# The vector engine parts weight blocks in place of POOL: RWKV projections and adding stages

## The chip, the cores and the metric

The kernel runs on one core of a Trainium2 chip. The metric is the device time of one execution in microseconds. The five engines of the core are named as in the profile: PE is TensorE, DVE the vector engine, ACT the scalar engine, POOL is GpSimd, SP issues DMAs.

## What is computed

Two blocks of a network, one after the other, in float32, for a sequence of 512 positions (`x`) and a context of 256 positions, 1024 channels wide. The first block mixes a gated linear recurrence with a chunked linear attention. The second has four layers: convolution, RWKV, attention, convolution. Each layer ends by adding a gated projection to the stream. What the change touches is matrix products `activations @ weights`, in the RWKV layer and at the layers' ends:

```
xx = centred_shift(h) - h
lerp = lambda n: h + xx * mu[n]
k = lerp(2) @ w_k
v = heads(lerp(3) @ w_v)
...
xw, xa = lerp(1), lerp(4)
...
r = heads(lerp(0) @ w_r) if with_out else None
g = (lerp(5) @ w_g) if with_out else None
...
x = x + gate[:, None] * y
```

## The kernel before

All activations lie transposed: channels on the 128 partitions, 8 tiles of 128 channels, positions along the free dimension (768 where stream and context go together, else 512). A weight block is one output tile's 1024x128 weights, laid out as 128x1024. The blocks are in one list in the order of use; SP brings them through a ring of four slots, each slot again as soon as the block in it is done with.

A product in float32 is made of three products of a narrower format (fp32r). Each weight block and each activation tile is split into a high and a low part. For a weight block this is done in two steps on two engines: ACT *rounds* it (`round_block`, a copy to fp32r, the high part), then another engine *parts* it (ring minus high part, the low part). The second step frees the block's ring slot (semaphore `parted`). There are two buffers of high and low weights (`PARTS["W"]`), used in turn. So block j+2 can be rounded when TensorE is done with block j (`blocks_done`), and it must be parted before TensorE comes to it, that is, while block j+1 runs. `tile_product` (one block) waits for `parted`, then issues 8 x 3 products, each in one or two matmuls of up to 512 columns.

POOL's form of the second step is `part_block` (line 437, instruction at L443), DVE's is `part_block_vector` (line 447, instruction recorded at the helper's line L361). A counter `done["part"]`, kept while the program is written, says which block comes next, whichever engine takes it. Before the change DVE parts the blocks of the convolution inputs and of attention, POOL most others.

Every engine works through its own instructions strictly in the order written. Each stage is a `Block`, whose end is a barrier of all engines. There is no scheduler: the order below is the order of the code.

**The adding stages** (`add_products`, line 1005; called for `out1`, `convout0`, `rwkvout` and `convout1`): eight output tiles, m = 0 to 7. TensorE makes tile m in one of two areas; DVE waits for it, adds it to the stream `X`, and sums squares for the next norm (`S.add`), which ACT makes in between (`S.square`). ACT rounds block m+2 when block m is done. POOL parts whatever is rounded, up to `limit`: to the stage's end and, but for `convout1`, two blocks of the next stage ahead. When all is added, ACT takes the logarithm and exponential of the norm (`S.root`), and the stage ends. `out1` and `convout1` are 512 wide, the other two 768.

**The RWKV projections** (stage `rkvg`, from line 1515): 34 blocks in six groups, each group with its own mix of the input: r (blocks 0 to 7), a low-rank pair `lora` w (8), k (9 to 16), `lora` a (17), v (18 to 25), g (26 to 33). The first two blocks are interleaved (`first_pair`). After each lora block and between the first blocks of k and v, TensorE makes small second products (`second`), which ACT evicts one by one. DVE first scales and shifts the input; then `differences()`, 8 pairs of a 512 and a 256 wide instruction; then for each further group n a pass of 16 mixing instructions (`lerp`), eight low parts of the activations (`low_part`), and in groups 1 and 4 a small addition (`mod_add`), which waits for TensorE to transpose a modulation (`mod_turn`), in group 4 after block 18:

```
for n in range(1, len(groups)):
    for k in range(DT):
        lerp(groups[n][0], k)
    for k in range(DT):
        low_part(n, k)
    v.wait_ge(h_split, DT * (n + 1))
    if n in (1, 4):
        mod_add(v, 5 + n // 4, MODS_7)
```

POOL has one call in this stage, `part_block(g, limit)` (line 1706): it parts every block as soon as ACT has rounded it. ACT rounds block t+1 just before it evicts block t.

Of the kernel before, what the change touches and what calls it, by code (L numbers as in the profile page):

```python
# [11 lines left out]
DT = D // P  # L12
# [149 lines left out]
PSTART = {n: sum(IS_SPLIT[:b]) for n, b in START.items()}  # L162
# [83 lines left out]
def two_blocks(nc, xT, pT, ctxT, vectors, consts, rope, weights, outT):  # L246
# [13 lines left out]
    with ctx:  # L260
# [20 lines left out]
        rounded, parted, direct_done, mod_done = sem("rounded"), sem("parted"), sem("direct_done"), sem("mod_done")  # L281
# [119 lines left out]
        def mod_add(v, third, col):  # L401

            layer, first = third // 3, third % 3 * DT
            v.wait_ge(mods_turned, third + 1)
            turned = PS[:, col:col + 2 * P].rearrange("p (h j q) -> p j h q", h=2, j=4)[:, :, :, 0:2]
            b = V("mod_b_2", 24 * layer + first, DT).rearrange("p (j h o) -> p j h o", h=2, o=1).broadcast_to([P, 4, 2, 2])
            o = MODL[:, layer, first:first + DT, :].rearrange("p (j h) v -> p j h v", h=2)
            vtt(o, turned, b, ALU.add).then_inc(mods_added, 1)
            v.wait_ge(mods_added, third + 1)
# [27 lines left out]
        def part_block(g, upto):  # L437

            while done["part"] < upto:
                j = done["part"]  # L440
                s = SPLIT_BLOCK[j] % SLOTS
                g.wait_ge(rounded, j + 1)
                nc.gpsimd.tensor_tensor(PARTS["W"][:, j % 2, 1, :], RINGT[:, s, :], PARTS["W"][:, j % 2, 0, :].bitcast(F32),  # L443
                                        ALU.subtract).then_inc(parted, 1)
                done["part"] += 1
# [559 lines left out]
        def add_products(stage, width, gate, ahead=2, split=None, mods=(), sums=None, bring=None, stream=None, splits_first=False, spill=False):  # L1005


            base_hi = next_use("split", DT) if split else 0
            base_low = next_use("low", DT) if split else 0
            halves = [(0, TX, 0), (TX, TT, 1)][:1 if width == TX else 2]  # L1010
            base = next_use("add", len(halves) * DT)
            limit = PSTART[stage] + DT + ahead
            S = Sums(width, *sums, lambda m: (freed_add, base + len(halves) * (m + 1)))
            with nc.Block() as block:
                @block.sync
                def _(sp):
                    if bring is not None:
                        bring(sp, base_hi)
                    R.supply(sp, RINGT, weights, min(b for b in [*START.values(), NB] if b > START[stage]) + SLOTS + 2)

                @block.scalar
                def _(a):
                    if split and not splits_first:
                        round_block(a, PSTART[stage] + 2)
                    if split:
                        split[0](a, base_hi, base_low)
                    if splits_first:
                        round_block(a, PSTART[stage] + 2)
                    a.preload_act_table_set(LN_EXP)

                    def square_and_spill(m):
                        S.square(a, m)
                        if spill:
                            a.dma_start(x_dram[:, m * TT:(m + 1) * TT], X[:, m, :]).then_inc(stores, 16)

                    for m in range(DT):
                        for third, col, rows, _n, _l, copy_at, _at in mods:
                            if m == copy_at:
                                mod_copy(a, third, col, rows)
                        round_block(a, PSTART[stage] + min(m + 3, DT))  # L1040
                        if m >= 1:
                            square_and_spill(m - 1)
                    square_and_spill(DT - 1)
                    round_block(a, limit)
                    S.root(a)

                entry = 2 if stage == "rwkvout" else 0
                done["part"] += entry

                @block.gpsimd  # L1050
                def _(g):
                    if entry:
                        g.wait_ge(parted, PSTART[stage] + entry)
                    part_block(g, limit)

                @block.tensor
                def _(pe):
                    for m in range(DT):
                        if m >= 2:
                            pe.wait_ge(freed_add, base + len(halves) * (m - 1))  # L1060
                        tile_product(pe, PS[:, (m % 2) * 1024:(m % 2) * 1024 + width], width,
                                     fresh=(split_low, base_low, 1) if split and m == 0 else None,
                                     mods=(*mods[0][3], mods[0][1]) if mods and m == 0 else (0, (), 0))
                        for third, col, rows, _n, later, _at, turn_at in mods:
                            if m in later:
                                mod_blocks(pe, 2, col)
                            if m == turn_at:
                                mod_turn(pe, third, col, rows)
                    S.total(pe)

                @block.vector
                def _(v):
                    for j in range(PSTART[stage], PSTART[stage] + entry):
                        v.wait_ge(rounded, j + 1)
                        vtt(PARTS["W"][:, j % 2, 1, :], RINGT[:, SPLIT_BLOCK[j] % SLOTS, :], PARTS["W"][:, j % 2, 0, :].bitcast(F32),
                            ALU.subtract).then_inc(parted, 1)
                    if split:
                        split[1](v, base_hi, base_low)
                    for m in range(DT):
                        if stream is not None:  # L1080
                            v.wait_ge(*stream(m))
                        v.wait_ge(blocks_done, PSTART[stage] + m + 1)
                        for a, b, c in halves:
                            p = PS[:, (m % 2) * 1024 + a:(m % 2) * 1024 + b]
                            if gate is None:
                                vtt(X[:, m, a:b], p, X[:, m, a:b], ALU.add).then_inc(freed_add, 1)
                            else:
                                stt(X[:, m, a:b], p, gate(m, c), X[:, m, a:b], ALU.mult, ALU.add).then_inc(freed_add, 1)
                        if m >= 2:
                            S.add(v, m - 1)  # L1090
                        for third, col, _rows, _n, _l, _at, turn_at in mods:
                            if m == turn_at:
                                mod_add(v, third, col)
                    S.add(v, DT - 1)

        add_products("out1", TX, None, split=plain_split([XC[:, k, :] for k in range(4)] + [O[:, k, :] for k in range(4)], TX),
                     mods=[(0, 4 * 512, RAW[:, 3, 0:256], (2, (3, 5)), (2, 4), 5, 6)],
# [439 lines left out]
        through = [sum(len(g[1]) for g in groups[:e]) for e in range(len(groups) + 1)]  # L1537
# [17 lines left out]
        limit = PSTART["rwkvout"]  # L1555
        in_loaded = [sem(f"in_loaded{q}") for q in range(8)]
        first_v = [s for s in seq if s[0] != "lora"].index(("v", 2, 0)) + 1
        with nc.Block() as block:
# [14 lines left out]
            def _(v):  # L1573
                def lerp(mu, k):
                    for a, b, c in HALF:
                        stt(LF[:, k, a:b], XX[:, k, a:b], V("rwkv_mu_2", mu * DT + k),
                            HP[:, k, hoff[c]:hoff[c] + b - a], ALU.mult, ALU.add).then_inc(l_ready, 1)
# [20 lines left out]

                def differences():
                    for k in range(DT):  # L1600
                        for a, b, c in HALF:
                            n, o = b - a, hoff[c]
                            dve_chain.inc(stt(XX[:, k, a:b], XX[:, k, a:b], 0.5, HP[:, k, o:o + n], ALU.mult, ALU.subtract))
                    dve_chain.wait(v)
# [17 lines left out]
                for n in range(1, len(groups)):  # L1622
                    for k in range(DT):
                        lerp(groups[n][0], k)
                    for k in range(DT):
                        low_part(n, k)
                    v.wait_ge(h_split, DT * (n + 1))
                    if n in (1, 4):
                        mod_add(v, 5 + n // 4, MODS_7)

            @block.tensor
            def _(pe):
# [38 lines left out]
                for e, (_mu, prods) in enumerate(groups):  # L1671
# [20 lines left out]
                    if prods[0][0] == "lora":  # L1692
# [7 lines left out]
                            pe.wait_ge(second_done[d], DT * q + HALF_M)  # L1700
                        pe.wait_ge(half_kept, q + 1)
                        pe.nop().then_inc(direct_done, 1)

            @block.gpsimd
            def _(g):
                part_block(g, limit)

            @block.scalar
            def _(a):
# [1450 lines left out]
```

## Time and profile before

| | |
|---|---|
| median of 3 runs | 2828.32 us (2817.24, 2828.32 and 3611.57) |
| the profiled execution | 2828.83 us |
| its span in the profile | 2827.0 us |
| mean granted clock of TensorE | 0.957 |
| busy: PE, DVE, ACT, POOL | 2518.5, 1516.1, 1100.2, 735.3 us |

The rest of the profile is a timeline in which each row is an instruction or a run of equal ones: start and length in us, engine, line, operation, tiles, shapes, count; in square brackets the engine's idle time just before it and what ended that. A run of equal rows is shown as one with its whole length. A weight block of a 768 wide stage is 48 matmuls. The granted clock is the share of 2.4 GHz that TensorE was given: 1.00 is 2.4 GHz, 0.50 is 1.2 GHz, and what lies between is a mean over a stretch that had both.

### The profile page before, as it was taken

To read this page: it belongs to the slowest core of one execution; us is meant where nothing else is said; L and a number is where in the kernel's file an instruction comes from. 1 tells how busy PE (TensorE), PEld (TensorE's weight loads), DVE (VectorE), ACT (ScalarE), POOL (GpSimd) and SP (SyncE) were. 2 spreads that over 40 slices of the span, in tenths; PEclk is the share of its full clock that TensorE was granted. 3 is DMA by queue.
4 is the path that set the end of the run, shared out by engine and by line. 5 is a ranking of instruction groups with operands and counts; after the bars stand their busy time and mean duration, and the time that the engine had idled before them with its cause. 6 is when DMAs were issued, how large, how long until landed. Compare 5 with 4: busy or idle time off the path is not lost. (4 is left out here: it accounts for less than half of the span.)

```text
span 2827.0 us, 66346 instructions
## 1 busy us (share of the span) xinstructions
PE 2518.5 (89%) x28704; PEld 1937.9 (69%) x28704; DVE 1516.1 (54%) x2491; ACT 1100.2 (39%) x1771; POOL 735.3 (26%) x422
## 2 busy tenths in 40 slices
PE   7998899999889995888888887889999999898987
PEld 5776577677667784777777776768788655475666
DVE  4734589863752213566666663444532466525975
ACT  4633321152443433444545543234422344423133
POOL 2422301422112225555545541200000000042132
PEclk9999999999899996999999999989999999998998
DMA  4224344424335531111111100633522100144432
GB/s 158 82 67 140 128 131 125 117 97 163 118 123 184 194 127 58 43 43 50 42 54 54 32 15 26 240 128 103 158 84 82 53 1 1 44 147 141 144 91 67
DMA packets 90286, 272.63 MB, mean 96 GB/s; under 512 B 13584, under 2 KB 14608, under 8 KB 89872
## 3 DMA queue, kind: packets, MB, share of 16 engines
q1 hardware_dynamic: 73872, 230.65, 25.4%
q10 hardware_dynamic: 16128, 37.76, 3.7%
q8 instruction: 230, 3.77, 0.6%
q14 instruction: 56, 0.46, 0.0%
HBM read 203.01 MB, written 36.70 MB: 85 GB/s over the span
## 5 line engine op out<-in xcount | busy, mean ns | idle before, releaser
L375 PE MATMUL ps<-h_parts_conv,w_parts_one 128*128 128x512 f32 x3168 | 582.0, 344 | 17.1 <-DVE h_parts_conv L361 11.8
L375 PEld LDWEIGHTS ps<-h_parts_conv,w_parts_one 128*128 128x128 f32 x3168 | 494.0, 191 | 108.1 <-issue 23.4
L375 PE MATMUL ps<-scratch_scan 64*64 64x64 f32 (+1 forms) x16704 | 384.6, 235 | 99.8 <-issue 60.1
L375 PEld LDWEIGHTS ps<-scratch_scan 64*64 64x64 f32 x16704 | 346.7, 137 | 143.9 <-issue 110.6
L372 ACT ACTIVATE scratch_scan<-ps 128x384 f32<-128x384 f32 x560 | 238.5, 495 | 336.5 <-PE ps L375 184.5
L443 POOL TENSOR_TENSOR w_parts_one<-ring,w_parts_one 128x1024 fp32r<-128x1024 f32 x83 | 208.1, 2509 | 583.6 <-ACT w_parts_one L372 583.4
L375 PE MATMUL ps<-h_parts_attn,w_parts_rwkv_out 128*128 128x512 f32 (+1 forms) x1536 | 329.2, 373 | 4.3 <-DVE h_parts_attn L369 4.3
L375 PEld LDWEIGHTS ps<-h_parts_attn,w_parts_rwkv_out 128*128 128x128 f32 x1536 | 263.2, 189 | 63.3 <-issue 9.1
L443 POOL TENSOR_TENSOR w_parts_rwkv_out<-ring,w_parts_rwkv_out 128x1024 fp32r<-128x1024 f32 x31 | 74.6, 2411 | 812.3 <-ACT w_parts_rwkv_out L372 812.3
L369 DVE SCALAR_TENSOR_TENSOR scratch_conv<-scratch_conv,vec 128x512 f32<-128x512 f32 (+1 forms) x408 | 252.4, 688 | 0.2
L372 ACT ACTIVATE scratch_conv<-ps 128x768 f32<-128x768 f32 (+2 forms) x90 | 65.0, 722 | 461.0 <-PE ps L375 461.0
L372 ACT ACTIVATE w_parts_rwkv_out<-ring 128x1024 fp32r<-128x1024 f32 x104 | 109.6, 1056 | 345.2 <-PE ps L375 324.8
L375 PE MATMUL ps<-h_parts_block,w_parts_one 128*128 128x512 f32 x960 | 236.5, 404 | 8.2 <-DVE h_parts_block L361 6.0
L375 PEld LDWEIGHTS ps<-h_parts_block,w_parts_one 128*128 128x128 f32 x960 | 182.7, 193 | 57.9 <-issue 8.2
L2601 POOL TENSOR_TENSOR scratch_scan<-scratch_scan,con 128x384 f32<-128x384 f32 x160 | 177.1, 1132 | 148.1 <-PE ps L375 140.5
L361 DVE TENSOR_TENSOR scratch_scan<-ps,scratch_scan 128x384 f32<-128x384 f32 (+1 forms) x272 | 127.5, 503 | 145.6 <-PE ps L375 115.3
L361 DVE TENSOR_TENSOR w_parts_rwkv_out<-ring,w_parts_rwkv_out 128x1024 fp32r<-128x1024 f32 x64 | 80.0, 1251 | 210.1 <-ACT w_parts_rwkv_out L372 210.0
L375 PE MATMUL ps<-h_parts_conv,w_parts_rwkv_out 128*128 128x512 f32 x768 | 185.6, 402 | 6.6 <-DVE h_parts_conv L361 3.4
L372 ACT ACTIVATE w_parts_one<-ring 128x1024 fp32r<-128x1024 f32 x106 | 111.6, 1055 | 188.0 <-PE ps L375 167.8
L375 PEld LDWEIGHTS ps<-h_parts_conv,w_parts_rwkv_out 128*128 128x128 f32 x768 | 146.3, 192 | 49.3 <-issue 17.5
L361 DVE TENSOR_TENSOR h_parts_conv<-scratch_conv,h_parts_conv 128x768 fp32r<-128x768 f32 (+1 forms) x64 | 62.3, 1021 | 170.6 <-ACT h_parts_conv L372 170.4
L361 DVE TENSOR_TENSOR scratch_conv<-scratch_conv 128x512 f32<-128x512 f32 (+1 forms) x124 | 114.4, 961 | 66.2 <-ACT scratch_conv L372 65.2
(219 smaller groups left out, 3262.4 us busy)
## 6 DMA issues: line engine op xcount, KB each, us to landing
ring<-in_weights SPq DMA_DIRECT2D x311, 512.0 KB, 3.7
rwkv_spill<-scratch_conv ACTq DMA_DIRECT2D x64, 384.0 KB, 2.3
stream<-rwkv_spill SPq DMA_DIRECT2D x64, 384.0 KB, 3.6
scratch_conv<-scratch_conv SPq DMA_DIRECT2D x128, 103.1 KB, 2.2
scratch_conv<-scratch_conv SPq DMA_DIRECT2D x128, 67.4 KB, 2.0
x_spill<-stream ACTq DMA_DIRECT2D x16, 384.0 KB, 2.5
kept_gate<-scratch_attn ACTq DMA_DIRECT2D x64, 64.0 KB, 2.6
y_spill<-scratch_scan SPq DMA_DIRECT2D x8, 384.0 KB, 2.7
```

The lines of the kernel that those rows point to most:

```text
L361: return nc.vector.tensor_tensor(o, a, b, op)
L369: return nc.vector.scalar_tensor_tensor(out=o, in0=a, scalar=s, in1=b, op0=op0, op1=op1)
L372: return nc.scalar.activation(o, a, f, **kw)
L375: return nc.tensor.matmul(o, l, r, start=start, stop=stop)
L443: nc.gpsimd.tensor_tensor(PARTS["W"][:, j % 2, 1, :], RINGT[:, s, :], PARTS["W"][:, j % 2, 0, :].bitcast(F32), ALU.subtract).then_inc(part ...
L2601: nc.gpsimd.tensor_tensor(NT[(NLV * w + lv) % 2][:, half(e), :].rearrange("p (j s) t -> p j s t", s=2), XX[:, aa_plane(w), 3 * e:3 * e + 3 ...
```

## The change

In `add_products` POOL now parts only what is left of the stage's first two blocks; DVE waits for these, parts block m+2 after it has added tile m and summed squares, and the blocks ahead at the end. In the RWKV stage POOL does nothing; DVE parts block 2 after five of the eight pairs of differences, then, after each pass of mixes, all blocks up to the first one of that group, and the last seven at the end. 62 parts move from POOL to DVE: 8 in `out1`, 8 in `convout0`, 32 in the RWKV stage, 8 in `rwkvout`, 6 in `convout1`. Blocks 0 and 1 of the RWKV stage are among those of `convout0`.

```diff
@@ add_products @@
                 @block.gpsimd
                 def _(g):
-                    if entry:
-                        g.wait_ge(parted, PSTART[stage] + entry)
-                    part_block(g, limit)
+                    part_block(g, PSTART[stage] + 2)
...
                     if split:
                         split[1](v, base_hi, base_low)
+                    v.wait_ge(parted, PSTART[stage] + 2)
                     for m in range(DT):
...
                         if m >= 2:
                             S.add(v, m - 1)
+                        part_block_vector(v, PSTART[stage] + min(m + 3, DT))
                         for third, col, _rows, _n, _l, _at, turn_at in mods:
                             if m == turn_at:
                                 mod_add(v, third, col)
                     S.add(v, DT - 1)
+                    part_block_vector(v, limit)
@@ the RWKV projections @@
                 def differences():
                     for k in range(DT):
+                        if k == 5:
+                            part_block_vector(v, PSTART["rkvg"] + 3)
                         for a, b, c in HALF:
...
                 for n in range(1, len(groups)):
                     for k in range(DT):
                         lerp(groups[n][0], k)
+                    part_block_vector(v, PSTART["rkvg"] + through[n] + 1)
                     for k in range(DT):
                         low_part(n, k)
                     v.wait_ge(h_split, DT * (n + 1))
                     if n in (1, 4):
                         mod_add(v, 5 + n // 4, MODS_7)
+                part_block_vector(v, limit)
...
-            @block.gpsimd
-            def _(g):
-                part_block(g, limit)
```

Where the parts now stand on DVE, first in the RWKV stage at the differences (`scratch_conv<-scratch_conv`, without `vec`) and the pass after them (with `vec`, of whose 16 rows the last two); the lines with + are new:

```order
 L369 SCALAR_TENSOR_TENSOR scratch_conv<-scratch_conv 128x512
 L369 SCALAR_TENSOR_TENSOR scratch_conv<-scratch_conv 128x256
+L361 TENSOR_TENSOR w_parts_one<-ring,w_parts_one 128x1024 [waits rounded_6]
 L369 SCALAR_TENSOR_TENSOR scratch_conv<-scratch_conv 128x512
 L369 SCALAR_TENSOR_TENSOR scratch_conv<-scratch_conv 128x256
@@ -664,4 +681,5 @@
 L369 SCALAR_TENSOR_TENSOR scratch_conv<-scratch_conv,vec 128x512
 L369 SCALAR_TENSOR_TENSOR scratch_conv<-scratch_conv,vec 128x256
+L361 TENSOR_TENSOR w_parts_one<-ring,w_parts_one 128x1024 [waits rounded_6] x6
 L361 TENSOR_TENSOR h_parts_conv<-scratch_conv,h_parts_conv 128x768 [waits hi_ready_79] x8
```

The first new row is block 2, the second blocks 3 to 8, which stand behind the whole pass of mixes and in front of the low parts of the next group.

On DVE at groups v and g of the RWKV stage, the end of one pass, the addition of the modulation (`mod`), and the end of the pass after it:

```order
 L369 SCALAR_TENSOR_TENSOR scratch_conv<-scratch_conv,vec 128x256
+L361 TENSOR_TENSOR w_parts_one<-ring,w_parts_one 128x1024 [waits rounded_6]
 L361 TENSOR_TENSOR h_parts_conv<-scratch_conv,h_parts_conv 128x768 [waits hi_ready_79] x8
 L361 TENSOR_TENSOR mod<-ps,vec 128x16 [waits mods_turned_11,h_split_80]
@@ -734,17 +755,20 @@
 L369 SCALAR_TENSOR_TENSOR scratch_conv<-scratch_conv,vec 128x512
 L369 SCALAR_TENSOR_TENSOR scratch_conv<-scratch_conv,vec 128x256
+L361 TENSOR_TENSOR w_parts_one<-ring,w_parts_one 128x1024 [waits rounded_6] x8
 L361 TENSOR_TENSOR h_parts_conv<-scratch_conv,h_parts_conv 128x768 [waits hi_ready_79] x8
```

Block 18 is parted before the addition of the modulation; blocks 19 to 26 come after it and after the next pass, where POOL had nothing in front of them.

On DVE at the end of `out1`, the last sums of squares, then the branch that ends the stage:

```order
 L361 TENSOR_TENSOR stream<-ps,stream 128x512 [waits blocks_done_5,mods_added_12]
 L361 TENSOR_TENSOR scratch_block<-scratch_block 128x512 [waits sq_used_19,sq_ready_18] x2
+L361 TENSOR_TENSOR w_parts_one<-ring,w_parts_one 128x1024 [waits rounded_6] x2
 L1014 UNCONDITIONAL_BRANCH
```

The two parts for the next stage are now the last work of DVE in this one.

## Rows read from the trace of the kernel before

**Rows 1.** The page's busy table: us (share of the span) xinstructions.

```profile
PE 2518.5 (89%) x28704; PEld 1937.9 (69%) x28704; DVE 1516.1 (54%) x2491; ACT 1100.2 (39%) x1771; POOL 735.3 (26%) x422
```

**Rows 2.** Groups by line: one part on POOL, one on DVE (mean ns).

```profile
L443 POOL TENSOR_TENSOR w_parts_one<-ring,w_parts_one 128x1024 fp32r<-128x1024 f32 x83 | 208.1, 2509 | 583.6 <-ACT w_parts_one L372 583.4
...
L361 DVE TENSOR_TENSOR w_parts_one<-ring,w_parts_one 128x1024 fp32r<-128x1024 f32 x14 | 17.1, 1221 | 0.6 <-ACT w_parts_one L372 0.5
```

**Rows 3.** Windows, RWKV projections: us, busy PE PEld DVE ACT POOL, clock, DMA.

```profile
704.70:1077.00 372.30, 339.24 (x1892) 273.41 (x1892) 133.07 (x201) 150.27 (x185) 82.56 (x32) 0.94 0.41 147
```

**Rows 4.** Timeline at block 10: DVE's third pass of mixes, block 10.

```profile
828.73 10.70 DVE L369 SCALAR_TENSOR_TENSOR scratch_conv<-scratch_conv,vec 128x512 f32<-128x512 f32 x16
...
837.58 8.65 PE L375 MATMUL ps<-h_parts_conv,w_parts_one 128*128 128x512 f32 x48
```

**Rows 5.** Timeline at blocks 1 to 3: differences, rounding, part, pass, block 2.

```profile
737.01 7.59 DVE L369 SCALAR_TENSOR_TENSOR scratch_conv<-scratch_conv 128x512 f32<-128x512 f32 x16
...
737.86 6.62 PE L375 MATMUL ps<-h_parts_conv,w_parts_one 128*128 128x512 f32 x36
...
741.57 1.06 ACT L372 ACTIVATE w_parts_one<-ring 128x1024 fp32r<-128x1024 f32 x1 [0.47 <-ACT scratch_conv L372]
...
742.71 4.12 POOL L443 TENSOR_TENSOR w_parts_one<-ring,w_parts_one 128x1024 fp32r<-128x1024 f32 x1 [38.80 <-ACT w_parts_one L372]
...
744.64 12.66 DVE L369 SCALAR_TENSOR_TENSOR scratch_conv<-scratch_conv,vec 128x512 f32<-128x512 f32 x16
...
746.97 10.17 PE L375 MATMUL ps<-h_parts_conv,w_parts_one 128*128 128x512 f32 x48 [2.48 <-POOL w_parts_one L443]
```

**Rows 6.** Windows (columns as rows 3): blocks 2, 3, 9 and 10.

```profile
747.00:757.00 10.00, 10.00 (x49) 8.63 (x50) 10.00 (x16) 0.00 (x0) 2.60 (x1) 0.83 0.38 113
757.00:766.00 9.00, 9.00 (x55) 7.92 (x53) 0.30 (x1) 2.10 (x3) 2.39 (x1) 1.00 0.30 102
...
826.20:836.10 9.90, 9.85 (x50) 8.41 (x50) 9.20 (x12) 4.12 (x5) 2.55 (x1) 0.86 0.64 214
...
837.60:846.10 8.50, 8.50 (x50) 7.30 (x48) 1.83 (x4) 2.87 (x3) 2.40 (x1) 1.00 0.37 141
```

**Rows 7.** Timeline at blocks 18 to 19: parts, modulation, last pass, block 19.

```profile
937.33 2.39 POOL L443 TENSOR_TENSOR w_parts_one<-ring,w_parts_one 128x1024 fp32r<-128x1024 f32 x1 [24.39 <-ACT w_parts_one L372]
...
942.34 0.17 DVE L361 TENSOR_TENSOR mod<-ps,vec 128x16 f32<-128x16 f32 x1 [7.63 <-PE ps L399]
942.55 8.56 DVE L369 SCALAR_TENSOR_TENSOR scratch_conv<-scratch_conv,vec 128x512 f32<-128x512 f32 x16
...
943.65 8.74 PE L375 MATMUL ps<-h_parts_conv,w_parts_one 128*128 128x512 f32 x48
...
947.62 5.74 POOL L443 TENSOR_TENSOR w_parts_one<-ring,w_parts_one 128x1024 fp32r<-128x1024 f32 x1 [7.89 <-ACT w_parts_one L372]
```

**Rows 8.** Timeline at block 16: TensorE's start.

```profile
898.18 17.19 PE L375 MATMUL ps<-h_parts_conv,w_parts_one 128*128 128x512 f32 x96 [0.32 <-POOL w_parts_one L443]
```

**Rows 9.** Timeline of `convout1`: a sum of squares on DVE, the next addition.

```profile
2792.99 2.49 DVE L361 TENSOR_TENSOR scratch_conv<-scratch_conv 128x512 f32<-128x512 f32 x1 [0.92 <-ACT scratch_conv L372]
2796.81 0.75 DVE L369 SCALAR_TENSOR_TENSOR stream<-ps,mod,stream 128x512 f32<-128x512 f32 x1 [1.33 <-PE ps L375]
```

**Rows 10.** Timeline at the end of `out1` and the next stage's start.

```profile
259.29 1.99 ACT L372 ACTIVATE w_parts_one<-ring 128x1024 fp32r<-128x1024 f32 x2
...
260.41 4.64 POOL L443 TENSOR_TENSOR w_parts_one<-ring,w_parts_one 128x1024 fp32r<-128x1024 f32 x2 [10.05 <-ACT w_parts_one L372]
...
262.03 0.58 ACT L372 ACTIVATE ps<-ps 128x512 f32<-128x512 f32 x1
...
265.85 2.06 DVE L369 SCALAR_TENSOR_TENSOR scratch_block<-stream,vec,ps 128x512 f32<-128x512 f32 x3 [5.73 <-PEq L1014]
...
268.68 1.08 PE L375 MATMUL ps<-ring,sc 128*32 128x256 f32 x8 [1.35 <-DMA ring<-in_weights]
```

**Rows 11.** Timeline at the end of `convout0`: POOL's last parts, ACT's last instruction.

```profile
699.25 4.65 POOL L443 TENSOR_TENSOR w_parts_one<-ring,w_parts_one 128x1024 fp32r<-128x1024 f32 x2 [17.86 <-ACT w_parts_one L372]
...
703.21 0.80 ACT L372 ACTIVATE ps<-ps 128x768 f32<-128x768 f32 x1
```

## The prediction

> **What bounds the kernel now.** I read the page's busy table first. TensorE is busy for 89% of the span [rows 1]. A change in who parts the weights is therefore worth only what it does to TensorE's own idle time, and to the ends of stages, where every engine waits for the slowest. The table of groups comes next. One part costs POOL 2509 ns and the vector engine (DVE) 1221 ns [rows 2]. That is 1.3 us less work for each of the 62 parts that move. In a stage that TensorE sets, though, a part need only be done before the block in front of it ends. So the third view is the timeline at the places where a part ends late, and where the vector engine has something long in front of the part that it is now handed. In the RWKV projections, which run from 704.7 to 1077 us, TensorE is busy for 339 of 372 us and the vector engine for 133 [rows 3]. The vector engine has room there; what it lacks is the right moment, because its queue is in order.
>
> **The change part by part.** Blocks of the RWKV stage are numbered from 0: r is 0 to 7, k 9 to 16, v 18 to 25, g 26 to 33, and 8 and 17 are the two low-rank blocks. A block takes 8.65 us at full clock [rows 4].
>
> *Block 2.* Before, ACT finished rounding it at 742.63, POOL started at 742.71 and needed 4.12 us, because it collided with the vector engine's work. TensorE, done with block 1 at 744.5, waited 2.48 us, and the block then took 10.17 us instead of 8.65 [rows 5]. The granted clock of that stretch is 0.83, a mixture of the 1.2 and 2.4 GHz levels, and 1.00 in the next [rows 6]. Now the vector engine reaches the part after five of its eight pairs of differences, 737.0 + 5 x 0.95 = 741.8. It waits for the rounding until 742.7 and ends at 742.7 + 1.25 = 743.95. (1.25 is my value for a part on the vector engine: 1.22 by the row and a little for a hop.) TensorE does not stop, and block 2 ends at 744.5 + 8.65 = 753.1 instead of 757.1: 4.0 us gained.
>
> *Block 3.* The gain is lost at once. Its part stands behind three pairs of differences (2.85 us) and the whole first pass of mixes, 16 instructions. Such a pass took 12.66 us here and 10.70 at block 10, where POOL parted at its start, but 8.56 at 942.55, where the vector engine kept going and POOL was the one held up, 5.74 us for one part [rows 4, 5, 7]. Without POOL in the stage I take 8.56. The part ends at 743.95 + 2.85 + 8.56 + 1.25 = 756.6; with 0.15 us to TensorE, as from POOL's end at 746.83 to the matmul at 746.97, block 3 starts at 756.8, after a wait of 3.7 us. I charge it the low clock that block 2 showed after 2.48 us, so 10.2 us instead of 8.65: it ends at 767.0, where before it ended at 757.1 + 8.65 = 765.8. Blocks 2 and 3 together: +1.2 us (-0.3 if the clock holds).
>
> The Trainium skill, "SBUF — State Buffer", section "SBUF: two separate sides", says that the vector engine and GpSimd contend for one port pair, which one of them holds for a whole instruction while the other stands still. The 5.74 us and 4.12 us parts agree. By that rule a pass is 8.56 us once POOL is gone, as in the sum; if the long passes had another cause, the sum is that of the first rival.
>
> *Block 10.* The third pass starts at 828.73 and now ends at 837.3, the part at 838.55, TensorE starts at 838.7 instead of 837.58 [rows 4]: +1.1 us. Whether a pause so short lowers the clock no row tells; between 0 and 1.5 us I take 0.
>
> *Block 16.* TensorE waited 0.32 us for POOL's part [rows 8]; that goes: -0.3 us.
>
> *Block 19* is the dear one. Before the last pass the vector engine adds a modulation that TensorE turns only after block 18, at 942.34. The pass of 16 follows, 942.55 to 951.1, and only then parts 19 to 26 [rows 7]. Before, POOL had that part ready before block 18 was over. Now it ends at 952.35 and TensorE starts block 19 at 952.5 instead of 943.65: +8.85 us, and +1.5 for the low clock after it. From block 20 on the vector engine has only parts in front of it and follows each rounding at once. ACT's rounding of block 20 does not wait for block 19, so nothing more is added.
>
> The sum for the stage: 1.2 + 1.1 - 0.3 + 10.35 = +12.35 us. Nothing after block 19 can take it back, since TensorE is continuous.
>
> *Block 8 and the other blocks* cost nothing. Their parts follow the rounding, or sit in front of low-part work that is paced by ACT. The cover is one block, 8.65 us; what comes first is 2 us of eviction and rounding and 1.25 of parting.
>
> *The adding stages* (the diff reaches four calls). In the two narrow ones a sum of squares now stands before the part; I read the last. It starts at 2792.99 and took 2.49 us against POOL [rows 9]. Even so the part would end at 2792.99 + 2.49 + 1.25 = 2796.73, and TensorE ends the block before 2796.81. The wide ones have over 3 us more. Cost 0; if the cover were missed in each of those twelve narrow parts by 0.5 us, 6 us.
>
> *Ends of stages.* After the first output projection POOL parts two blocks ahead, 260.41 to 265.05, while ACT is done at 262.61; the next stage's vector work starts at 265.85 [rows 10]. Now the two parts end at 261.65 and 262.9 (the second rounding ends at 261.28), so that stage starts 2.15 us earlier. Its first transfers also wait for these parts to free ring slots: TensorE's wait for DMA before 268.68 moves with them. -2.15 us. At the end of the next such stage POOL is done at 703.90 and ACT at 704.01 [rows 11]: 0. The RWKV output stage ends in the same way: 0. The last parts nothing ahead: 0.
>
> In all +12.35 - 2.15 = +10.2 us. The profiled execution took 2828.83 us (span 2827.0), half a microsecond above the median of the runs shown, 2828.32, so I add to it: 2839.0 us.
>
> **The rivals.** (1) *The long passes are not POOL's doing.* The first would stay at 12.66 us and the others at 10.70. Block 3 would be 4.1 us later, block 10 and block 19 each 2.1 later: +8.3, 2847.3 us. For it: the long passes are the more frequent. Against it: a pass has the same 16 instructions each time, and only the collision differs.
>
> (2) *TensorE doesn't wait in the RWKV stage*, because the parts come in time after all: then only the gains are left, 2.15 + 4.0 + 0.3 = 6.45, 2822.4 us. For it: the vector engine is idle for nearly two thirds of the stage. Against it: the two passes stand in front of parts 3 and 19 in one queue, and their start and length are read, not guessed. The Trainium skill speaks for this rival: "Perfetto Trace Analysis", section "Optimizing Scalar/DVE Operations", would move work off the vector engine if that is saturated, and it is not, at 133 of 372 us. By that rule alone the time is the 2822 of this rival; I think a busy share can't tell when one part is due.
>
> (3) *Slower beyond doubt: the clock does not come back.* If after the wait at block 19 TensorE stayed at 1.2 GHz to the end of the stage, its 15 blocks would take up to 8.65 us more each: +130, some 2967 us. It passes 2% from the sixth such block. Against it: after the pauses of the low-rank part the stretch 826.2 to 836.1 was granted 0.86, and 837.6 to 846.1 was at 1.00 again [rows 6].
>
> **How the numbers follow.** The forecast, 2839.0, has a chance of 0.72. Its own range comes from the clock terms (-3, +1.5, and as much again if the low stretch after the long wait is longer) and from the spread of the runs shown without the outlier, 11 us: 2829 to 2849. Rival 1 has 0.12, rival 2 0.13, rival 3 0.02, and 0.01 is left for anything else. The range of eight in ten takes in rival 1 whole with its spread and reaches to rival 2: 2822 to 2853. A measurement of this kernel tells some 2% from no change, 57 us. Only rival 3 and a disturbance reach that: faster 0.01, same 0.97, slower 0.02.
>
> **What would show it.** In the profile of the changed kernel: no wait of TensorE at block 2; a wait of 3 to 4 us before block 3 and of nearly 9 before block 19, both ended by the vector engine's part; passes of 8.6 us each; about 1 us at block 10; the stage after the first output projection 2 us earlier; granted clock under 1.00 just after the two long waits and 1.00 after that. Passes over 10 us would make it rival 1; no wait at block 19, or one ended by something other than the vector engine, would make the main term wrong.

## The result, and the profile after

The changed kernel takes 2832.07 us (median of 20 runs, 2823.56 to 2835.79), the kernel before 2820.56 us (20 runs, one of them the 3611.57 us shown ahead). The ratio is 1.0034, 95% interval 1.0025 to 1.0043: 9.6 us slower, within the 2% that count as the same. The ratios here are not quotients of the two medians and differ from them by up to 0.0007; the medians of this pair lie 11.5 us apart. The forecast was 10.2 us slower. The changed kernel's profiled execution took 2835.79 us with a span of 2833.9.

The page's busy table of the changed kernel, against [rows 1]:

```profile
PE 2519.4 (89%) x28704; PEld 1940.8 (68%) x28704; DVE 1551.0 (55%) x2553; ACT 1099.2 (39%) x1771; POOL 583.9 (21%) x360
```

POOL has 62 instructions and 151 us less, the vector engine 62 instructions and 35 us more. By busy time that is a good trade: it frees 116 us of engine time. The groups by line say the same of each part, against [rows 2]. (The 62 of this row are its 14 of before and 48 of the moved parts; the other 14 moved parts stand under another name of the buffer, `w_parts_rwkv_out`, so the two sixty-twos agree by chance.)

```profile
L361 DVE TENSOR_TENSOR w_parts_one<-ring,w_parts_one 128x1024 fp32r<-128x1024 f32 x62 | 75.5, 1224 | 190.2 <-ACT w_parts_one L372 190.2
```

The loss is in none of these numbers. It is in TensorE's waits. Among TensorE's waits, added up by what ended them (us in total, times, longest), these are the rows on this buffer's parts, first of the kernel before, then of the changed one:

```profile
PE ps L375 <- POOL w_parts_one L443: 4.9, 3, 2.5
```

```profile
PE ps L375 <- DVE w_parts_one L361: 14.3, 3, 8.7
PE ps L375 <- POOL w_parts_one L443: 2.1, 1, 2.1
```

Two short waits for POOL are gone (2.48 us at block 2 and 0.32 us at block 16), and three for the vector engine have come, 14.3 us together, the longest 8.7. The timeline of TensorE and the vector engine at the first of them, against [rows 5]:

```profile
734.17 14.92 PE L375 MATMUL ps<-h_parts_conv,w_parts_one 128*128 128x512 f32 x84
...
738.94 1.23 DVE L361 TENSOR_TENSOR w_parts_one<-ring,w_parts_one 128x1024 fp32r<-128x1024 f32 x1 [0.83 <-ACT w_parts_one L372]
740.08 2.90 DVE L369 SCALAR_TENSOR_TENSOR scratch_conv<-scratch_conv 128x512 f32<-128x512 f32 x6
743.01 8.57 DVE L369 SCALAR_TENSOR_TENSOR scratch_conv<-scratch_conv,vec 128x512 f32<-128x512 f32 x16
...
751.49 2.36 DVE L361 TENSOR_TENSOR w_parts_one<-ring,w_parts_one 128x1024 fp32r<-128x1024 f32 x2
752.86 22.48 PE L375 MATMUL ps<-h_parts_conv,w_parts_one 128*128 128x512 f32 x117 [3.56 <-DVE w_parts_one L361]
```

The first part is block 2's, done at 740.17; TensorE goes from block 1 to block 2 without a pause (one run of 84 matmuls). On the vector engine there follow three pairs of differences and the pass of 16, with no instruction between, and only then block 3's part. The second place, against [rows 4], and the third, against [rows 7]:

```profile
825.70 8.72 PE L375 MATMUL ps<-h_parts_conv,w_parts_one 128*128 128x512 f32 x48 [0.29 <-PE ps L375]
...
828.18 8.57 DVE L369 SCALAR_TENSOR_TENSOR scratch_conv<-scratch_conv,vec 128x512 f32<-128x512 f32 x16
...
836.66 1.22 DVE L361 TENSOR_TENSOR w_parts_one<-ring,w_parts_one 128x1024 fp32r<-128x1024 f32 x1
838.02 10.24 PE L375 MATMUL ps<-h_parts_conv,w_parts_one 128*128 128x512 f32 x48 [2.12 <-DVE w_parts_one L361]
...
936.36 1.06 ACT L372 ACTIVATE w_parts_one<-ring 128x1024 fp32r<-128x1024 f32 x1 [0.46 <-ACT scratch_conv L372]
...
942.56 0.17 DVE L361 TENSOR_TENSOR mod<-ps,vec 128x16 f32<-128x16 f32 x1 [7.68 <-PE ps L399]
942.77 8.56 DVE L369 SCALAR_TENSOR_TENSOR scratch_conv<-scratch_conv,vec 128x512 f32<-128x512 f32 x16
951.24 2.36 DVE L361 TENSOR_TENSOR w_parts_one<-ring,w_parts_one 128x1024 fp32r<-128x1024 f32 x2
952.61 11.49 PE L375 MATMUL ps<-h_parts_conv,w_parts_one 128*128 128x512 f32 x48 [8.67 <-DVE w_parts_one L361]
```

Note that the vector engine stood idle for 7.68 us just before the modulation at 942.56. ACT had rounded block 19 by 937.42, so its part could have been done in that time; it stood behind the modulation and the pass in the queue. The windows at these places (us, busy PE PEld DVE ACT POOL, granted clock, DMA), against [rows 6]: the stretch behind each wait is below full clock, the next one is at 1.00 again.

```profile
752.00:763.00 11.00, 10.14 (x49) 8.84 (x50) 1.85 (x2) 0.00 (x0) 0.00 (x0) 0.84 0.31 97
763.00:790.00 27.00, 27.00 (x154) 23.51 (x153) 3.69 (x3) 6.60 (x8) 0.00 (x0) 1.00 0.31 103
...
838.00:849.00 11.00, 10.98 (x64) 9.00 (x64) 1.23 (x1) 1.95 (x3) 0.00 (x0) 0.84 0.38 110
849.00:870.00 21.00, 21.00 (x130) 16.41 (x126) 2.45 (x2) 7.01 (x9) 0.00 (x0) 1.00 0.58 213
...
952.00:965.00 13.00, 12.39 (x54) 10.18 (x55) 1.61 (x2) 0.81 (x1) 0.00 (x0) 0.74 0.24 81
965.00:1010.00 45.00, 45.00 (x255) 37.34 (x252) 6.13 (x5) 13.95 (x15) 0.00 (x0) 1.00 0.59 216
```

The gain is at the end of the first output projection, against [rows 10]: the two parts end at 260.10 where POOL's ended at 265.05, and the next stage's vector work starts 5.50 us after the last addition (255.40 to 260.90), not 7.82 (258.03 to 265.85). First the last addition before, then the rows of the changed kernel:

```profile
258.03 0.69 DVE L361 TENSOR_TENSOR stream<-ps,stream 128x512 f32<-128x512 f32 x1 [4.42 <-PE ps L375]
```

```profile
255.40 0.69 DVE L361 TENSOR_TENSOR stream<-ps,stream 128x512 f32<-128x512 f32 x1 [4.42 <-PE ps L375]
...
257.74 2.36 DVE L361 TENSOR_TENSOR w_parts_one<-ring,w_parts_one 128x1024 fp32r<-128x1024 f32 x2 [0.25 <-ACT w_parts_one L372]
...
259.40 0.58 ACT L372 ACTIVATE ps<-ps 128x512 f32<-128x512 f32 x1
260.90 2.06 DVE L369 SCALAR_TENSOR_TENSOR scratch_block<-stream,vec,ps 128x512 f32<-128x512 f32 x3 [0.80 <-PEq L1014]
```

### The profile page after: what moved, and what is told of

Its sections match the earlier page's. It is cut to its first block and busy times, and to the rows that moved or that the text cites. A ratio compares the mean times of both kernels' runs of the same rounds, so it can differ in the third digit from the quotient of the medians.

```text
span 2833.9 us, 66348 instructions
## 1 busy us (share of the span) xinstructions
PE 2519.4 (89%) x28704; PEld 1940.8 (68%) x28704; DVE 1551.0 (55%) x2553; ACT 1099.2 (39%) x1771; POOL 583.9 (21%) x360
## 5 line engine op out<-in xcount | busy, mean ns | idle before, releaser
L375 PE MATMUL ps<-h_parts_conv,w_parts_one 128*128 128x512 f32 x3168 | 585.8, 346 | 29.0 <-DVE w_parts_one L361 14.3
L375 PEld LDWEIGHTS ps<-scratch_scan 64*64 64x64 f32 x16704 | 346.9, 137 | 140.2 <-issue 106.7
L369 DVE SCALAR_TENSOR_TENSOR scratch_conv<-scratch_conv,vec 128x512 f32<-128x512 f32 (+1 forms) x408 | 240.2, 660 | 0.2
L361 DVE TENSOR_TENSOR w_parts_rwkv_out<-ring,w_parts_rwkv_out 128x1024 fp32r<-128x1024 f32 x78 | 97.0, 1246 | 214.0 <-ACT w_parts_rwkv_out L372 213.8
L443 POOL TENSOR_TENSOR w_parts_rwkv_out<-ring,w_parts_rwkv_out 128x1024 fp32r<-128x1024 f32 x17 | 41.1, 2420 | 811.2 <-ACT w_parts_rwkv_out L372 811.2
L361 DVE TENSOR_TENSOR w_parts_one<-ring,w_parts_one 128x1024 fp32r<-128x1024 f32 x62 | 75.5, 1224 | 190.2 <-ACT w_parts_one L372 190.2
L443 POOL TENSOR_TENSOR w_parts_one<-ring,w_parts_one 128x1024 fp32r<-128x1024 f32 x35 | 87.6, 2504 | 265.2 <-ACT w_parts_one L372 265.1
L361 DVE TENSOR_TENSOR scratch_conv<-scratch_conv 128x512 f32<-128x512 f32 (+1 forms) x124 | 102.8, 868 | 67.1 <-ACT scratch_conv L372 65.7
```

The source lines that it names most:

```text
L361: return nc.vector.tensor_tensor(o, a, b, op)
L369: return nc.vector.scalar_tensor_tensor(out=o, in0=a, scalar=s, in1=b, op0=op0, op1=op1)
L375: return nc.tensor.matmul(o, l, r, start=start, stop=stop)
```

## The experiments

Two theories were put to the test. *The queue's order*: only three of the moved parts cost anything, those of blocks 3, 10 and 19, because each stands behind a pass in an in-order queue at the moment when it is due. (Those of blocks 9 and 18 stand behind a pass too, but were not late.) *The load*: the vector engine is simply busier, and the cost is spread over all moved parts by their number.

A measured ratio has an interval of 2.5 to 6 us either way, and single executions differ by more than that in stages that nothing here touches (below). So beside each ratio stands the length of the RWKV stage in the profiled execution, from the start of ACT's rounding of block 0 to that of block 33. Its three sections are cut at the roundings of blocks 10 and 19; a rounding begins when the block two before it is done, so the sections hold blocks 0 to 8, 9 to 17 and 18 to 31.

| kernel | ratio to before (95%) | RWKV stage, us | blocks 0-8 | 9-17 | 18-31 |
|---|---|---|---|---|---|
| before | 1 | 362.4 | 132.0 | 106.0 | 124.3 |
| changed | 1.0034 (1.0025 to 1.0043) | 377.5 | 134.9 | 106.7 | 135.9 |
| changed, again | 1.0047 (1.0031 to 1.0063) | 378.2 | 134.9 | 109.0 | 134.4 |
| RWKV stage alone | 1.0053 (1.0035 to 1.0072) | 375.5 | 134.2 | 106.8 | 134.6 |
| adding stages alone | 0.9997 (0.9985 to 1.0010) | 360.8 | 133.7 | 104.5 | 122.6 |
| block 19 early | 0.9991 (0.9977 to 1.0006) | 364.0 | 132.4 | 108.4 | 123.3 |
| block 19 early, again | 1.0004 (0.9994 to 1.0014) | 364.4 | 134.5 | 106.7 | 123.3 |
| three early | 0.9983 (0.9972 to 0.9995) | 357.0 | 128.6 | 105.3 | 123.0 |
| three early, again | 0.9977 (0.9963 to 0.9991) | 355.7 | 128.6 | 102.8 | 124.3 |
| each part twice | 1.0079 (1.0057 to 1.0101) | 381.4 | 137.7 | 110.3 | 133.4 |
| each part twice, again | 1.0073 (1.0053 to 1.0093) | 382.3 | 137.7 | 109.6 | 135.0 |

### The two halves of the change

The first kernel gives the adding stages back to POOL, the second the RWKV stage.

```diff
  RWKV stage alone, against the changed kernel:
-                    part_block(g, PSTART[stage] + 2)
+                    if entry:
+                        g.wait_ge(parted, PSTART[stage] + entry)
+                    part_block(g, limit)
...
-                    v.wait_ge(parted, PSTART[stage] + 2)
...
-                        part_block_vector(v, PSTART[stage] + min(m + 3, DT))
...
-                    part_block_vector(v, limit)
```

```diff
  adding stages alone, against the changed kernel:
-                        if k == 5:
-                            part_block_vector(v, PSTART["rkvg"] + 3)
...
-                    part_block_vector(v, PSTART["rkvg"] + through[n] + 1)
...
-                part_block_vector(v, limit)
+
+            @block.gpsimd
+            def _(g):
+                part_block(g, limit)
```

> Only the 32 weight blocks of the RWKV projections are parted by VectorE; the five adding stages stay on POOL. Theory of the queue's order (three parts, of blocks 3, 10 and 19, stand in VectorE's queue behind a pass of 8.56 us, and TensorE waits for them; all else is hidden; the adding stages gain at out1's end): the change costs more without the adding stages' gain: 12 to 14 us over the kernel before, ratio 1.0043 to 1.0050, the waits of 3.6, 2.1 and 8.7 us before blocks 3, 10 and 19 all there. Rival (the cost is VectorE's load, shared by all 62 parts by their number): 32 of 62 of 9.6 us, 5 us, ratio 1.0018.

Measured: 1.0053, 15 us on 2817.6. The waits are there: 3.56, 1.97 and 8.67 us. The ratio is just over the first theory's range, which its interval holds; the rival's 1.0018 lies outside.

> Only the 30 weight blocks of the five adding stages are parted by VectorE; the RWKV projections stay on POOL. Theory of the queue's order: a gain of 2.3 us at the end of out1 and up to 2 us more if the 2 us earlier start of the attention stage, seen in one profile of the changed kernel, is the change's doing and not the clock's: 2 to 4.5 us below the kernel before, ratio 0.9984 to 0.9993. Rival (load by the number of parts): 30 of 62 of 9.6 us, 4.6 us over it, ratio 1.0016.

Measured: 0.9997, interval 0.9985 to 1.0010. The rival's 1.0016 is outside it. The first theory's range, 0.9984 to 0.9993, is missed too, by about 1 us, and by time alone no gain is shown, since the interval holds 1. The gain at out1's end is in the profile, with the same start of the next stage, 0.80 us after TensorE's release:

```profile
262.18 2.36 DVE L361 TENSOR_TENSOR w_parts_one<-ring,w_parts_one 128x1024 fp32r<-128x1024 f32 x2 [0.25 <-ACT w_parts_one L372]
265.35 2.07 DVE L369 SCALAR_TENSOR_TENSOR scratch_block<-stream,vec,ps 128x512 f32<-128x512 f32 x3 [0.80 <-PEq L1014]
```

In all eleven profiles the stretch from out1 to the next stage (between two of ACT's roundings) is 65.9 us where POOL has the adding stages' parts and 63.6 where the vector engine has them: 2.3 us. The further 2 us that I allowed for, an earlier start of the attention stage, is hardly the change's: the kernel that leaves those stages on POOL shows 1.5 us of it too (168.9 us from the RWKV output stage to there, 170.4 before, 167.8 to 169.1 in the others). Without those 2 us I would have said 0.9992, inside the interval.

### One part moved ahead of its pass

If the place in the queue is what costs, the same instruction on the same engine must cost nothing in another place.

```diff
                     for k in range(DT):
                         low_part(n, k)
                     v.wait_ge(h_split, DT * (n + 1))
+                    if n == 4:
+                        part_block_vector(v, PSTART["rkvg"] + through[n] + 2)
                     if n in (1, 4):
                         mod_add(v, 5 + n // 4, MODS_7)
```

> The changed kernel, with the part of block 19 put ahead of the 5th group's modulation addition and pass in VectorE's queue. Theory of the queue's order: the wait of 8.7 us before block 19 goes and with it the slow block behind it (11.49 against 8.74 us): 11 us below the changed kernel, so 1 to 3 us below the kernel before, ratio 0.9990 to 0.9997. Rival (load): as many parts on VectorE, so nothing changes: ratio 1.0034.

Measured: 0.9991, and in a second set of runs 1.0004. The wait before block 19 is gone. In the second profile:

```profile
939.61 1.23 DVE L361 TENSOR_TENSOR w_parts_one<-ring,w_parts_one 128x1024 fp32r<-128x1024 f32 x1 [2.65 <-ACT w_parts_one L372]
943.48 0.17 DVE L361 TENSOR_TENSOR mod<-ps,vec 128x16 f32<-128x16 f32 x1 [2.65 <-PE ps L399]
943.69 8.56 DVE L369 SCALAR_TENSOR_TENSOR scratch_conv<-scratch_conv,vec 128x512 f32<-128x512 f32 x16
944.87 8.73 PE L375 MATMUL ps<-h_parts_conv,w_parts_one 128*128 128x512 f32 x48
```

The part fits into the vector engine's idle time before the modulation, the pass still takes 8.56 us, and block 19 runs at full clock with no wait. The section with block 19 is 123.3 us in both, against 134.4 to 135.9: 11 us and more, for one instruction that moved past 17 others. A load theory has no place for this.

> The same kernel as the one with block 19's part early, beside the next. Theory of the queue's order: 11 us below the changed kernel, ratio 0.9990 to 0.9997; in the trace no wait before block 19. Rival (load): 1.0034.

The first ratio lies in the range, the second above it, though its interval (0.9994 to 1.0014) reaches into it. The wait before block 3 is still there in both profiles (3.40 us). Before block 10 it is 1.82 us in the second; in the first TensorE came later, after a slow block 9 (9.96 us), and waited 1.01 us for ACT. These waits stand against out1's gain.

### The other two parts moved into their passes

```diff
                     for k in range(DT):
                         lerp(groups[n][0], k)
+                        if (n, k) in ((1, 1), (3, 3)):
+                            part_block_vector(v, PSTART["rkvg"] + (4 if n == 1 else through[n - 1] + 2))
```

> The same, and also the parts of blocks 3 and 10 are put between the instructions of the pass that they stood behind (after its 2nd of 8 row blocks, and after its 4th). Theory of the queue's order: the waits of 3.6 and 2.1 us go too, with 2 to 4 us of slow clock behind them, while the pass itself ends 1.2 us later, which nothing waits for: 6 to 9 us below the kernel with block 19 alone mended, so 8 to 11 us below the kernel before, ratio 0.9961 to 0.9972. Rival (load): nothing changes, ratio 1.0034.

Measured: 0.9983, outside the range (its interval, 0.9972 to 0.9995, touches it). That is less gain than I expected, and only 3 us under the kernel with block 19's part alone early in medians. The RWKV stage of the profile was 7 us shorter, though, so both were run again side by side.

> The same kernel as the one with all three parts early, beside the one with block 19's alone. The first pair gave a difference of 3 us in the medians, where the traces of that pair showed 7 us less in the RWKV stage. Theory of the queue's order: 4 to 8 us below the kernel with block 19's part alone early, ratio to the kernel before 0.9970 to 0.9985. If the waits before blocks 3 and 10 are given back later in the stage, the two kernels are equal within 2 us.

Measured: 0.9977, 6.5 us below the kernel with block 19's part alone early (2812.41 and 2818.91 us) and 6.4 below the kernel before (2818.83). In the timeline of the first of the two profiles the part of block 3 is between four and twelve instructions of the pass, and TensorE shows no wait from block 1 on:

```profile
735.48 14.92 PE L375 MATMUL ps<-h_parts_conv,w_parts_one 128*128 128x512 f32 x84
...
744.33 2.21 DVE L369 SCALAR_TENSOR_TENSOR scratch_conv<-scratch_conv,vec 128x512 f32<-128x512 f32 x4
746.46 1.22 DVE L361 TENSOR_TENSOR w_parts_one<-ring,w_parts_one 128x1024 fp32r<-128x1024 f32 x1
747.59 6.44 DVE L369 SCALAR_TENSOR_TENSOR scratch_conv<-scratch_conv,vec 128x512 f32<-128x512 f32 x12
...
750.38 24.86 PE L375 MATMUL ps<-h_parts_conv,w_parts_one 128*128 128x512 f32 x139
```

The whole stage is 356.4 us (mean of two) against 361.6 for the two kernels that leave it to POOL. This is the version that beats both: it keeps the gains at block 2 and at out1's end, and pays none of the three waits.

### Twice the load, nothing moved

Here the load is doubled and the order kept: each part is done twice, the second copy releasing TensorE.

```diff
+                if PSTART["rkvg"] <= j < PSTART["rwkvout"]:
+                    dlink(vtt(PARTS["W"][:, j % 2, 1, :], RINGT[:, s, :], PARTS["W"][:, j % 2, 0, :].bitcast(F32), ALU.subtract))
                 vtt(PARTS["W"][:, j % 2, 1, :], RINGT[:, s, :], PARTS["W"][:, j % 2, 0, :].bitcast(F32), ALU.subtract).then_inc(parted, 1)
```

> The changed kernel, with each of the 34 parts of the RWKV projections done twice by VectorE, one copy behind the other, the second alone releasing TensorE. Theory of the queue's order: VectorE has room for 34 more parts of 1.22 us, and only the three that stand behind a pass are seen by TensorE: each wait grows by 1.3 us, the one before block 3 by up to 2.6 us (block 2's second copy also holds up the pass): 4 to 6 us above the changed kernel, ratio to the kernel before 1.0048 to 1.0055. Rival (load): all 34 second copies are paid, 42 to 44 us above the changed kernel, ratio 1.018 to 1.019.

Measured: 1.0079, above the first theory's range, which the interval (1.0057 to 1.0101) just leaves out, and far under the rival's. Five runs are few, so it ran again beside the changed kernel.

> The changed kernel itself, beside the next, on one chip. Ratio to the kernel before 1.0034 as measured first, by either theory.

> The same kernel with each part of the RWKV projections done twice. Its first profile had the RWKV stage 3.8 us longer than the changed kernel's, its first times 12 us more, from five undisturbed runs. Theory of the queue's order, by the profile: 4 to 6 us above the changed kernel beside it, ratio 1.0048 to 1.0055. If the second copies cost more than the three waits show, 10 us or more above it, ratio 1.007 or more. Rival (load): 42 us above it.

Measured: 1.0047 for the changed kernel, 1.0073 for this one: 7 us between them by the ratios, 9.7 by the medians. That is above the 4 to 6 us of the first theory, and the ratio fits the second alternative, that the copies cost more than the three waits show. The 42 us of the load theory are nowhere near. The windows of the RWKV stage show what was absorbed, the changed kernel's first profile, then the second of this one:

```profile
704.00:1077.00 373.00, 329.49 (x1800) 265.99 (x1801) 154.37 (x222) 146.97 (x181) 0.00 (x0) 0.93 0.40 143
```

```profile
704.00:1077.00 373.00, 325.39 (x1791) 260.43 (x1792) 193.30 (x263) 146.72 (x181) 0.00 (x0) 0.92 0.41 142
```

The vector engine has 39 us more to do in that window, and the stage grew by 4.0 us (mean of two against mean of two). What grew is the waits, here in the timeline of that second profile:

```profile
744.37 8.69 PE L375 MATMUL ps<-h_parts_conv,w_parts_one 128*128 128x512 f32 x48 [0.86 <-DVE w_parts_one L361]
...
758.18 53.43 PE L375 MATMUL ps<-h_parts_conv,w_parts_one 128*128 128x512 f32 x288 [4.89 <-DVE w_parts_one L361]
...
844.39 10.17 PE L375 MATMUL ps<-h_parts_conv,w_parts_one 128*128 128x512 f32 x48 [3.01 <-DVE w_parts_one L361]
...
906.63 16.98 PE L375 MATMUL ps<-h_parts_conv,w_parts_one 128*128 128x512 f32 x96 [0.42 <-DVE w_parts_one L361]
...
960.88 10.37 PE L375 MATMUL ps<-h_parts_conv,w_parts_one 128*128 128x512 f32 x48 [9.93 <-DVE w_parts_one L361]
```

Block 3's is now 4.89 (3.56), block 10's 3.01 (2.12), block 19's 9.93 (8.67). Two short ones are new: 0.86 at block 2 and 0.42 at block 16. The second copies of blocks 0 and 1 stand at the end of convout0; there they end after ACT's last instruction, and block 2 is rounded 0.4 us later after block 0 than in the changed kernel, which is part of the 4.0 us. So second copies are paid where the part is due at once, and the others are hidden.

Both ratios, 1.0079 and 1.0073, are some 8 us above what these 4 us would add to the changed kernel's first ratio, and some 4 us above what they would add to its second. In the profiles the rest lies in code that is the same in both kernels, and not twice in one place: in the first pair the RWKV stage begins 4.8 us later, in the second the scan, the stage behind it, is 7.6 us longer. That speaks for chance, but it is not shown.

## Why the prediction was right

*The whole.* 9.6 us by the ratio, 11.5 by the medians, against 10.2. It was right for its reason: the waits are ended by the vector engine's parts, at the three blocks named, and they go when the parts move. Part of the closeness is luck, though. By the stage lengths the RWKV stage costs 15.5 us (377.1, the mean of the three profiles with its parts on the vector engine in the changed place, less 361.6, the mean of the two on POOL), not 12.35. Less 2.3 us at out1's end that makes 13; the first set of runs puts the change at 7 to 12 us, the second at 9 to 18. Two terms were too small, as told below: the low clock behind block 10 and behind block 19. With them the terms add up to 14.9 us in the first profile of the changed kernel. The stretches between, where TensorE waits for a part only at block 16 and there for 0.8 us at most, vary by themselves: in the eleven profiles blocks 4 to 8 took 62.8 to 65.2 us and blocks 11 to 17 took 82.9 to 86.0, whoever parts the weights. In that profile they gave +2.1 and, beside block 16's term, -1.6. The absolute time, 2839.0, came out 7 us high, because the profiled execution to which I added was itself 8 us above the median of more runs (2828.83 against 2820.56).

*Blocks 2 and 3.* Right. Block 2 has no wait; block 3 waits 3.56 us (forecast 3.7). From the starts of ACT's roundings, block 2 gains 4.29 us (forecast 4.0), and block 3 gives back 5.40: together +1.1 (forecast +1.2).

*The first rival* falls. All five passes of the changed kernel take 8.56 or 8.57 us; the one beside POOL's part of block 2 took 12.66 and that at block 10 took 10.70 [rows 4, 5], and with the stage given back to POOL (adding stages alone) they take 12.66 and 10.71 again. The trace agrees with the rule of the Trainium skill on the shared port pair ("SBUF — State Buffer", section "SBUF: two separate sides"): with POOL gone from the stage, nothing holds a pass up.

*Block 10* was mis-sized. The step that failed is "Whether a pause so short lowers the clock no row tells; between 0 and 1.5 us I take 0." The pause was 2.12 us, since block 9 ran at full clock this time (8.72 us, 9.91 before) and TensorE came 1.2 us sooner; and block 10 then took 10.24 us instead of 8.65. The pair of blocks cost +2.6 us in this profile (-1.20 and +3.80), not +1.1. My bound held, my choice within it did not.

*Block 16.* Right: no wait there any more.

*Block 19.* The wait is 8.67 us (forecast 8.85). The clock behind it cost more: the block took 11.49 us, 2.75 over its 8.74, where I charged 1.5. In the other two profiles with this wait it took 10.01 and 10.95. In all +11.49 against +10.35 forecast. From block 20 on nothing is added, as forecast.

*The second rival* falls by the same rows: TensorE waited, with the vector engine 41% busy (154 of 373 us). The doubled parts show that its premise was true and still beside the point: there was room for 39 us more at a price of 4, but not at the moment when the part was due. The rule of the Trainium skill that was quoted for it ("Perfetto Trace Analysis", section "Optimizing Scalar/DVE Operations") asks whether the engine is saturated. The prediction left out that the same section also names Scalar and Vector engines that are not saturated and still cause bubbles on others; the trace agrees with that: an engine 41% busy made TensorE wait 14.3 us.

*The third rival* falls: the stretch after each wait's block is granted 1.00.

*Ends of stages.* out1's end gains 2.32 us (forecast 2.15). The ends of convout0 and of the RWKV output stage cost and gain next to nothing, as forecast, and TensorE's waits in the changed kernel have no row on a moved part outside those three.

## What to carry to other kernels

Before work is moved to an engine with an in-order queue, write down for each moved instruction what stands ahead of it there and when it is due; the engine's busy share does not answer that. The dear ones can be few (here 3 of 62), and here they could be put ahead of the long piece, or between its instructions, where TensorE no longer waits for them. After such a mend the move was worth 0.2%; as it was made it cost 0.3 to 0.5%.

## What was not expected

*The same pause, two lengths of the block behind it.* After waits of 1.82 and 1.97 us block 10 took 8.71 us, at a granted clock of 1.00; after 2.09 and 2.12 us it took 10.17 and 10.24, at 0.83. A wait of 8.67 us was followed by blocks of 10.01 to 11.49 us, at 0.85 down to 0.73, one of 9.93 us by blocks of 10.07 and 10.37. So the price of a late part is its wait and 0 to 2.75 us on top, and I know of no row that says which.

*A stage that nothing touches varies by 11 us.* From ACT's last rounding in the RWKV stage to its first after the scan, the profiles show 701.6 to 712.5 us, with 712.2 in the kernel before and 701.8 in the one whose RWKV stage is the same as before. That is more than the whole effect of the change, so one profile set against another says nothing of it unless it is read stage by stage. What makes the scan longer or shorter was not tried.
